# The opening of a two-layer hybrid decoder step on one core: input in four pieces over two request queues, squares on VectorE, products of ones on TensorE

## The reference, cut to what matters

```python
def rmsnorm(x, gain):
    xf = x.astype(jnp.float32)
    y = xf * lax.rsqrt(jnp.mean(xf * xf, axis=-1, keepdims=True) + RMS_EPS)
    return (y * gain.astype(jnp.float32)).astype(x.dtype)
def swiglu(x, w_gate, w_up, w_down):
    return (jax.nn.silu(x @ w_gate) * (x @ w_up)) @ w_down
...
    x = x + 0.5 * swiglu(rmsnorm(x, ffn1_norm), ffn1_w_gate, ffn1_w_up, ffn1_w_down)
    z = rmsnorm(x, mix_norm) @ w_in
```

## Time and profile before

| | |
|---|---|
| median of 3 runs | 1161.28 us |
| the profiled execution: its own time | 1161.36 us |
| its span, first to last instruction | 1159.3 us |
| TensorE (PE) busy | 1148.5 us, 99% of the span, 7914 matmuls |
| POOL, DVE, ACT busy | 806.0, 598.5, 532.8 us |
| share of the DMA engines in use by the queue of SP | 49.8% |
| mean granted clock | 1.000 |

### The profile page before, as it was taken

How to read it: one execution, slowest core, us unless ns; L and a number is a source line. 1 busy time by engine, 2 the same in 40 slices (tenths; PEclk the granted TensorE clock), 3 DMA queues, 4 the chain that set the end, 5 groups by cost and what they waited for, 6 DMA issues and landing times.

```text
span 1159.3 us, 22766 instructions
## 1 busy us (share of the span) xinstructions
PE 1148.5 (99%) x7914; PEld 1132.1 (98%) x7914; DVE 598.5 (52%) x878; ACT 532.8 (46%) x801; POOL 806.0 (70%) x421
## 2 busy tenths in 40 slices
PE   7999999999999999999999999999999999999999
PEld 6999999999899999999999999999998999999998
DVE  5865562239967544432258655522598764444100
ACT  5444444444765444444444444444457654444332
POOL 6776667777776766667667766677786776666674
DMA  8444445557535544445565444455573654443453
GB/s 295 153 162 146 145 118 149 149 171 221 159 120 165 173 146 154 143 122 148 159 196 161 147 146 146 119 149 162 179 211 114 183 154 153 152 152 124 138 149 107
DMA packets 72203, 180.91 MB, mean 156 GB/s; under 512 B 10210, under 2 KB 25826, under 8 KB 72162
## 3 DMA queue, kind: packets, MB, share of 16 engines
q1 hardware_dynamic: 71680, 179.23, 49.8%
q10 hardware_dynamic: 482, 1.16, 0.3%
HBM read 176.78 MB, written 3.58 MB: 156 GB/s over the span
## 4 chain that ended last, share of the span: by engine, by line
PE 96%; DMA 1%; DVE 1%; ACT 1%; POOL 0%; issue 0%; SPq 0%; DVEq 0%
PE bank L611 28%; PE bank L614 28%; PE bank L612 28%; PE bank L897 2%; PE bank L899 2%; PE bank L898 2%; PE bank L671 1%; PE bank L672 1%; PE bank L670 1%; DMA x<-in_xT 1%; DMA raw<-in_w 0%; PE bank L879 0%; PE bank L857 0%; PE bank L732 0%; PE bank L839 0%; POOL w_lo L506 0%
## 5 line engine op out<-in xcount | busy, mean ns | idle before, releaser
L506 POOL TENSOR_TENSOR w_lo<-raw,w_hi 128x1024 fp32r<-128x1024 f32 (+2 forms) x351 | 766.5, 2189 | 321.0 <-ACT w_hi L985 320.5
L985 ACT ACTIVATE w_hi<-raw 128x1024 fp32r<-128x1024 f32 (+2 forms) x351 | 336.5, 961 | 439.2 <-PE bank L614 423.2
L611 PE MATMUL bank<-xg_hi,w_hi 128*128 128x320 f32 x1552 | 481.8, 310 | 0.9 <-DVE tmp L1264 0.9
L614 PE MATMUL bank<-xg_hi,w_lo 128*128 128x320 f32 x1552 | 479.6, 309 | 0.0
L612 PE MATMUL bank<-xg_lo,w_hi 128*128 128x320 f32 x1552 | 479.5, 309 | 0.0
L611 PEld LDWEIGHTS bank<-xg_hi,w_hi 128*128 128x128 f32 x1552 | 291.3, 188 | 3.7 <-issue 1.9
L612 PEld LDWEIGHTS bank<-xg_lo,w_hi 128*128 128x128 f32 x1552 | 291.4, 188 | 0.4
L614 PEld LDWEIGHTS bank<-xg_hi,w_lo 128*128 128x128 f32 x1552 | 291.3, 188 | 0.0
L611 PE MATMUL bank<-h_hi,w_hi 128*128 128x320 f32 x704 | 217.5, 309 | 0.0
L612 PE MATMUL bank<-h_lo,w_hi 128*128 128x320 f32 x704 | 217.5, 309 | 0.0
L614 PE MATMUL bank<-h_hi,w_lo 128*128 128x320 f32 x704 | 217.5, 309 | 0.0
(11 more groups left out here) (188 smaller groups left out, 816.6 us busy)
## 6 DMA issues: line engine op xcount, KB each, us to landing
raw<-in_w SPq DMA_DIRECT2D x223, 512.0 KB, 3.8
raw<-in_w SPq DMA_DIRECT2D x64, 384.0 KB, 3.0
raw<-in_w SPq DMA_DIRECT2D x64, 320.0 KB, 2.9
k_all<-in_cache_kT SPq DMA_DIRECT2D x32, 128.0 KB, 3.5
v_past<-in_cache_v SPq DMA_DIRECT2D x32, 128.0 KB, 2.8
cst<-in_consts ACTq DMA_DIRECT2D x1, 997.0 KB
out_yT<-x SPq DMA_DIRECT2D x1, 960.0 KB, 4.9
x<-in_xT SPq DMA_DIRECT2D x2, 320.0 KB, 3.8
```

The costliest lines, as they stand in the source:

```text
L506: pool.tensor_tensor(w_lo[:, j, 0:count * P], raw[:, j, 0:count * P], w_hi[:, j, 0:count * P].bitcast(F32), ALU.subtract).then_inc(split.s ...
L611: pe.matmul(out, hi, in_hi[:, k, :], start=first and n == 0, stop=False)
L614: mm = pe.matmul(out, lo, in_hi[:, k, :], start=False, stop=last and end)
L985: act.activation(w_hi[:, j, 0:count * P], raw[:, j, 0:count * P], ACT.Copy).then_inc(split_hi.sem, 1)
```

## The change

In words:

1. The input comes in four pieces of two tiles (320 KB each), first on the queue of SP. The gains and both halves of slot 0 are requested by ACT, on a queue of its own.
2. SP requests slot 0 of the second iteration ahead of the seven small loads.
3. TensorE multiplies ones by ones (128x128, float32, into bank 5, which nobody reads): 12 times ahead of the first product, and once behind each of the first six high products of slot 0. DVE sets `ones` first of all.
4. DVE squares tiles 0 to 3, 6 and 7, and ACT tiles 4 and 5. ACT rounds slot 1 before it squares.
5. In place of the reduction DVE adds the squares one by one: seven adds, each waiting for the one before, in PSUM (`square_sum`, in bank 7) except the last, which writes `sumsq`.
6. The product of ones with `sumsq` stands behind slot 1 in place of slot 2, and ACT takes the root ahead of rounding slots 0 and 1 of the second iteration.

```diff
-X_PIECES = ((0, 2), (2, 4), (4, 8))
+X_PIECES = ((0, 2), (2, 4), (4, 6), (6, 8))
...
-            sp.dma_start(gain[:, :], gains).then_inc(gain_in.sem, 16)
...
-            load_x(0)
-            sp.dma_start(raw[:, 0, 0:HALF], slot_0[:, 0:HALF]).then_inc(half_in.sem, 16)
-            load_x(1)
-            sp.dma_start(raw[:, 0, HALF:2 * HALF], slot_0[:, HALF:2 * HALF]).then_inc(raw_in[0].sem, 16)
-            load_x(2)
+            for n in range(len(X_PIECES)):
+                load_x(n)
             for j in range(1, 4):
                 load_slot(0, BASE_G1, 0, j, w8, W8_G1, HALVES8)
+            load_slot(0, BASE_G1, 1, 0, w8, W8_G1 + 1, HALVES8)
...
+            def idle_products(count):
+                for _ in range(count):
+                    pe.matmul(bank[5][:, 0:P], ones[:, :], ones[:, :], start=True, stop=True)
...
+                    if j == 0 and k < 6:
+                        idle_products(1)
...
+                        pe.wait_ge(ones_ok.sem, 1)
+                        idle_products(WARM_PRODUCTS)
                         first_part(j, range(0, 4), half_hi.sem, 1, half_lo.sem, 1)
...
-                    if j == 2:
+                    if j == 1:
                         sum_squares(0, 0)
...
+            act.dma_start(gain[:, :], gains).then_inc(gain_in.sem, 16)
+            act.dma_start(raw[:, 0, 0:HALF], slot_0[:, 0:HALF]).then_inc(half_in.sem, 16)
+            act.dma_start(raw[:, 0, HALF:2 * HALF], slot_0[:, HALF:2 * HALF]).then_inc(raw_in[0].sem, 16)
...
-            for d in range(DT // 2, DT):
-                dve.tensor_tensor(tmp[:, d, :], x[:, d, :], x[:, d, :], ALU.mult).then_inc(squared_too.sem, 1)
-            dve.wait_ge(squared_first.sem, DT // 2)
-            dve.wait_ge(squared_too.sem, DT // 2)
-            dve.tensor_reduce(sumsq[:, :], tmp[:, :, :].rearrange("p d t -> p t d"), AX.X, ALU.add).then_inc(summed.sem, DT)
+                for d in range(*piece) if n < 2 else ():
+                    squares_too(d)
+            for d in range(6, 8):
+                squares_too(d)
+            add_squares(square_sum, tmp[:, 0, :], tmp[:, 1, :], 6).then_inc(squared_too.sem, 1)
+            for n, d in enumerate((2, 3, 6, 7)):
+                add_squares(square_sum, square_sum, tmp[:, d, :], 7 + n).then_inc(squared_too.sem, 1)
+            dve.wait_ge(squared_first.sem, 2)
+            add_squares(square_sum, square_sum, tmp[:, 4, :], 11).then_inc(squared_too.sem, 1)
+            add_squares(sumsq[:, :], square_sum, tmp[:, 5, :], 12).then_inc(summed.sem, DT)
```

More of the change, by code:

```diff
@@ L449, in load_x @@
                 sp.dma_start(x[:, piece, :], xT[:, piece, :]).then_inc(x_in[n].sem, 16)
-            load_x(0)
-            sp.dma_start(raw[:, 0, 0:HALF], slot_0[:, 0:HALF]).then_inc(half_in.sem, 16)
-            load_x(1)
-            sp.dma_start(raw[:, 0, HALF:2 * HALF], slot_0[:, HALF:2 * HALF]).then_inc(raw_in[0].sem, 16)
-            load_x(2)
+            for n in range(len(X_PIECES)):
+                load_x(n)
             for j in range(1, 4):
                 load_slot(0, BASE_G1, 0, j, w8, W8_G1, HALVES8)
+            load_slot(0, BASE_G1, 1, 0, w8, W8_G1 + 1, HALVES8)
             for L in range(DEPTH):
                 load_small(L)
-                with sp.Fori(1, IT_G) as i:
+                for j in range(0 if L else 1, 4):
+                    load_slot(L, BASE_G1, 1, j, w8, L * W8_ROWS + W8_G1 + 1, HALVES8)
+                with sp.Fori(2, IT_G) as i:
                     load(L, BASE_G1, i, w8, L * W8_ROWS + W8_G1 + i, HALVES8)
@@ L1076, in _ @@
             round_first(1, raw_in[0].sem)
-            for d in range(DT // 2 - 2):
+            round_piece(2)
+            round_piece(3)
+            round_slot(0, BASE_G1, 0, 1, HALVES8)
+            for d in range(4, 6):
                 square_first(d)
[L1079 to L1082, removed]
+            for j in range(2, 4):
                 round_slot(0, BASE_G1, 0, j, HALVES8)
@@ L1227, in _ @@
             dve.sem_inc(taken.sem, 4)
-            for n, (ap, value) in enumerate(((stat[:, 42:43], 1.0), (stat[:, 60:61], RMS_EPS), (stat[:, 61:62], LN_EPS), (ones[:, :], 1.0), (q_pad[:, :, :, :], 0.0),
+            dve.memset(ones[:, :], 1.0).then_inc(ones_ok.sem, 1)
+            for n, (ap, value) in enumerate(((stat[:, 42:43], 1.0), (stat[:, 60:61], RMS_EPS), (stat[:, 61:62], LN_EPS), (q_pad[:, :, :, :], 0.0),
                                              (conv_in[:, :, 0:CONV_HIST], 0.0), (pool_in[:, :, 0:POOL_HIST], 0.0))):
@@ L1293, in residual, with squares_too, add_squares @@
                     add_square(d, square[:, d % 2, :], L * (3 * DT) + d + (norm - 1) * DT, L * summed.per + d + norm * DT)
+            def squares_too(d):
+                dve.tensor_tensor(tmp[:, d, :], x[:, d, :], x[:, d, :], ALU.mult).then_inc(squared_too.sem, 1)
+            def add_squares(out, a, b, count):
+                dve.wait_ge(squared_too.sem, count)
+                return dve.tensor_tensor(out, a, b, ALU.add)
             for n, piece in enumerate(X_PIECES):
```

9 lines of the change are left out of this document (4 added, 5 removed).

## The result

The changed kernel takes **1168.24 us**, the median of 4 runs (1167.72 to 1168.84), against 1161.27 for the kernel before: 1.0059 times as long, with an interval of 1.0047 to 1.0071. Forecast were 1160.8 us and a range from 1158.0 to 1162.4. It is slower by 7.0 us, three times what a measurement can tell from no change. The profiled execution took 1168.84 us, 7.5 more than the one before, with a span of 1167.1.

A forecast was written before the change was run, and what follows sets the result against it. TensorE, busy nearly throughout, bounds the kernel, so only its second iteration's start counts: 26.55 - 27.02 = -0.5 us, other edits at nothing. From the median 1161.28 that gives 1160.8 us; range 1158.0 to 1162.4 for 8 in 10.

The forecast's parts named there:

- Low parts follow as before: Opening, DVE: the input's low parts come behind ACT's rounding as in the kernel before, with no added cost.
- T: Opening, ACT: the time when all input tiles are rounded, put at 11.45 us (12.45 before).
- the port is lost twice: Rival: square 7 waits for POOL's split of slot 1, the first add for slot 2's; 1163.1 us, chance 0.07.
- The stretch that counts: Only TensorE's start of its second iteration, 27.02 us before, makes the kernel shorter or longer.
- x at 10.45, slot 1 at 11.75: Opening input: x complete at 10.45 us; ACT rounds slot 1 at about 11.75 us (13.07 before).
- The rival in which two queues move more bytes: Rival on the input: x at 9 us, the rest as forecast; 1159.4 us, chance 0.07.
- The price of the adds: DVE's sum of squares: 0.55 us for each add, six of them 3.3 us; the first add priced apart.
- The first add against POOL, then 2.5 us for the sum: The first add waits for POOL's split of slot 1, until 15.7; TensorE waits 2.5 us until 19.0.
- the first rival: The first add gets in before POOL; second iteration at 24.5 us, 2.5 us faster, 1158.8 us; chance 0.29.
- The second iteration at 26.55: TensorE: sum ready at 19.0, product of ones 0.54, 48 matmuls 7.05 us; start at 26.55, before 27.02.
- Bank 0's wait of 1.07 us: TensorE's wait before its second iteration, 1.07 us: gone, with the root at about 19.8 and bank 0 taken by 22.9.
- The clock: Rival: TensorE's clock falls in the 2.5 us wait for the sum, costing 2.9 us; 1163.7 us, chance 0.04.

The follow-up runs named there:

- the first wait on POOL: The changed kernel with POOL held back from its split of slot 1 until all eight low parts are made: 1162.44 us.
- the second wait on POOL: The changed kernel with POOL held back from its split of slot 1 until DVE has made the first add: 1160.84 us.
- The pair of edits: The kernel before with edits 1, 2, 4 and 5 together: 1165.96 us.
- the root between the roundings: The kernel before with edits 4 and 5, and ACT's root between its rounding of slots 0 and 1 of the second iteration: 1160.31 us.

## Why the prediction was wrong

**The step that failed** is the last sentence on the input, "Low parts follow as before", with T as their only condition. Nowhere in the sum did DVE's squares of tiles 0 to 3 have a place or a price. They stand ahead of the low parts of the next tiles. As measured, squares 0 and 1 took 1.97 us in place of 0.88 beside POOL's first half, low parts 2 and 3 took 2.01 beside the second, and low part 4 started 2.5 us behind ACT's rounding, not 0.7. There POOL's split of slot 1 met it, and three of the last four low parts waited for a split each. T itself was right, 11.45 us; what it didn't fix was when the low parts followed. The forecast had squares 6 and 7 ended at 12.95; they ended at 21.13.

**The rule was right, its use too narrow.** From the earlier trace rows I had taken that a DVE instruction with two operands in SBUF waits for POOL's split, and priced one such instruction, the first add. The four low parts just ahead of it are of the same kind, and so are the squares. The rival "the port is lost twice" counted two losses and 1163.1 us; it could be lost once for every instruction of that kind while POOL has work. The Trainium skill, "SBUF — State Buffer", section "SBUF: two separate sides", says of the port pair that the two engines share that whichever instruction starts first gets it "for the whole instruction; the other fully blocks". The runs agree on the blocking: 2.60 us for an add of 0.50, 8.23 for four low parts of 1.94. Who is first can't be read from the starts alone: with the first wait on POOL its split starts at 13.88 us, yet the square that starts at 14.12 ran in 0.48 and the split took 3.00 in place of 2.38. The runs also settle what no row had shown: that the add's result goes to PSUM doesn't free it.

**Point by point.**
- *The stretch that counts* (the second iteration's start): right; 7.9 us there, 7.8 in the span.
- *x at 10.45, slot 1 at 11.75*: too late by 1.0 and 0.4 us (x at 9.4; rounded from 11.36). T came out at 11.45 all the same, since ACT rounded four tiles behind slot 0's half and not two behind the last landing; that part was luck. From 7 to 9 us the engines moved 412 GB/s against 378, and the last piece was requested 0.95 us earlier; which of the two made it is not separated. It also varies: in the profiled executions with these requests ACT rounds tile 4 at 8.46 to 9.65 us. The rival in which two queues move more bytes has about this input, though not its earlier T, and its 1159.4 is as wrong as the forecast, for the same missing step.
- *The price of the adds*: right. Five take 2.71 us, 0.54 each where I had 0.55.
- *The first add against POOL, then 2.5 us for the sum*: not in this kernel, where the splits were through at 19.97, before the add; shown as forecast in three others (2.58 to 2.60 us; waits for the sum of 1.2, 2.2 and 2.3). So both signs that I had set for the first rival were there, seven adds near 0.5 us and no wait for the sum, in a kernel 7 us slower: it was the splits that were over, not the add that came first.
- *The second iteration at 26.55*: its terms, 19.0, 0.54 and 7.05, add up to 26.59, which changes nothing.
- *Bank 0's wait of 1.07 us goes*: right.
- *Ones at nothing*: right, by the runs with them alone and with them away.
- *Late gains* had no place in the sum. They moved ACT's first rounding to 5.82 us, and cost nothing, as the run with the gains first shows.
- *The clock*: I gave its fall 0.04 and placed it in the wait for the sum. In the profiled execution of the change it fell between 12 and 14 us (granted 0.63 there, 0.50 in the next 2 us), when TensorE had just waited for the low parts whose products start at 9.94 and 11.42 us. It cost 1.9 us in slot 1 and 0.5 in the last four products of slot 0 (1.06 us for 0.59), which the account above has in slot 0's 7.0.

**What stays open.** When the clock falls is not settled. With a wait of 2.2 us for the sum and POOL held back it stayed at 1.00; with 2.3 us on the kernel before with edits 4 to 6 it fell. With the second wait on POOL, TensorE's waits ahead of 12 us were 1.1, 0.2 and 1.1 us, nearly the 1.2, 0.4 and 1.1 of the changed kernel, and it stayed at 1.00. In the changed kernel with the old requests it was 0.50 from 11.9 to 15.3 us, behind a wait of 1.8 us for the input. It probably makes part of the spread between executions. The pair of edits took 1168.8 us in its profiled execution, where slot 1's products are 0.267 us apart although the column prints 1.00, and 1165.6 to 1166.1 in the others, which have no trace. And whether the second wait on POOL and the root between the roundings add up wasn't tried.

## What to carry to other kernels

When work is moved to VectorE, write down for every VectorE instruction around it how many operands it reads from SBUF and what GpSimd runs at that time: each one with two can pay a whole GpSimd instruction, and in a chain one after the other pays, as long as GpSimd has work. A transfer that comes earlier also starts the engine behind it earlier, and that may be the one that blocks. Where such a meeting can't be avoided, one wait that holds the long instruction back until the short ones are through is cheap: here 0.5 us of waiting gave back 7.

## What the runs showed of the hardware that I had not expected

- DVE and POOL alternate once both have work at hand: back-to-back DVE instructions with two SBUF operands don't keep the turn. Of four low parts one took 0.54 us and three 2.63 to 2.66, the two splits in between 2.59 and 2.60 in place of 2.38. Where POOL only joins, one more DVE instruction can still go first: with the first wait on POOL a square did that started 0.24 us behind the split.
- A request of 28 KB took 3.6 us to land while pieces of 320 KB were requested on the other queue. With the gains first on SP's queue they took 2.0 us, and ACT's table load behind them began at 2.83 us in place of 4.52.
- The granted clock fell to 0.50 at 12.5 us behind waits of 1.2, 0.4 and 1.1 us, without one long wait; behind nearly the same waits it stayed at 1.00 in the run with the second wait on POOL.
